# Eight weight slots and a third Strassen pair in a two-layer float32 trunk

## The chip, the core and the metric

The kernel runs on one core of one Trainium2 chip. Its time is that of the device in microseconds; lower is better. A core has TensorE (PE, matrix products), VectorE (DVE), ScalarE (ACT), GpSimd (POOL, nearly idle here) and SyncE (SP, which issues nearly all DMAs here). Each engine works through its own instructions in order and waits on semaphores that others raise.

## The reference

Two layers on x of 256 tokens by 2048, all in float32. Layer 0 mixes tokens by sparse attention, layer 1 by a short gated convolution, and each has a SwiGLU block behind it:

```python
for i in range(DEPTH):                       # DEPTH = 2
    if i % 2 == 0:
        x = x + _dsa_mixer(_rmsnorm(x, attn_norm[j]), attn_w_in[j], ..., attn_w_out[j])
    else:
        x = x + _shortconv_mixer(_rmsnorm(x, conv_norm[j]), conv_w_in[j], conv_w[j], conv_w_out[j])
    x = x + _swiglu(_rmsnorm(x, ffn_norm[i]), ffn_w_gate[i], ffn_w_up[i], ffn_w_down[i])

def _swiglu(h, w_gate, w_up, w_down):
    return (jax.nn.silu(h @ w_gate) * (h @ w_up)) @ w_down
```

w_gate and w_up are 2048 x 5632, w_down is 5632 x 2048. The weights make up nearly all of the 398 MB that are read from memory.

## The kernel before

**A float32 product in three.** Every operand is split in a high part (a rounding to the type float32r) and a low part (what is left). A product is then high x high + high x low + low x high: three matmuls of 128 x 128 on 512 columns (`product`, L726 to L728; `stream_rows`, L502 to L504, in the projections). ACT makes a weight's high part w_hi (L931), DVE its low part w_lo (L1282).

**Slots.** Weights come in slots of 128 partitions x 1024 numbers (512 KB), which is two row tiles of 512 columns. SP loads a slot into `stage`, ACT and DVE split it into w_hi and w_lo, PE uses it. All three buffers have RING = 4 places. SP may load slot n when slot n-4 has its low part (`lo_done`); ACT may write w_hi of slot n when PE is done with slot n-4 (`slot_used`).

**Units of gate and up.** A SwiGLU block has 11 units of 512 hidden columns (BLOCKS). A unit has eight pairs of slots, kp = 0 to 7; the even slot holds two row tiles of w_gate, the odd one the same rows of w_up. A plain pair (`plain_slot`, twice) is 2 slots x 2 token halves x 2 row tiles x 3 = 24 matmuls. The sums stand in the eight banks of PSUM, named P1 to P8. Units 1 to 10 are a loop on every engine.

**Mixed pairs.** Pairs 3 and 6 (MIXED_PAIRS) are done by a Strassen form: seven products in place of eight, so 21 matmuls (`mixed_pair`). Four of the products take the slots themselves, three take sums of weight quarters. DVE makes these sums from `stage` into t_raw with four subtractions (`mix_weights`, L1612 to L1617; the second, L1613, writes into `stage`), ACT makes t_hi (L1164), DVE t_lo (L1622, semaphore `t_ready`). t_raw, t_hi and t_lo exist once: the next mix waits for `t_used`, which PE raises with the pair's last product. The mixed inputs lie in sx, two sets, in the last four tiles of hs; they are made once a layer, from quarter j of the residual (`mix_x`, `mixed_x_high`, `mixed_x_low`).

**End of a unit.** During slots 0 to 3 of the next unit, ACT takes P1, DVE adds up the mixed sums (`take_mixed`, L1566), then gate (L1581) and up (L1586) rows, ACT does silu, DVE the product (`hid`, L1593). PE transposes the hidden block between slots 2 and 3 into banks 6 and 7 (`turn_hidden`, L536), which are also the banks P6 and P7 of the mixed pairs. ACT and DVE bring it as high and low part into hs (L1157, L1600, semaphore `hidden_ready`).

**Down.** Two passes of 44 slots on w_down, pairs 6, 9, 12, 15, 18 mixed. In the first pass the mixed forms of the hidden blocks are made as well, one set every six slots, behind t_lo: DVE (L1669 to L1678), ACT (L1196, L1198), DVE (L1684, L1685).

The order on every engine is written out by hand: `unit_slots` goes through the slots, and a table of steps says what follows a slot's split.

Of the kernel before, what the change touches and what calls it, by code (L numbers as in the profile page):

```python
# [32 lines left out]
P = 128  # L33
# [9 lines left out]
RING = 4  # L43
SLOT = 1024
# [21 lines left out]

def trunk(nc, x, attn_w_in, attn_w_out, conv_w_in, conv_w_out, w_gate, w_up, w_down,
          gains, head_gains, conv_taps, tables, mats, bounds, out):
    with ExitStack() as ctx:
# [7 lines left out]
        stage = sb("stage", [P, RING, SLOT])  # L77
# [6 lines left out]
        taps = sb("taps", [P, 3, KT])  # L84
        mat = sb("mat", [P, 2, P])
# [19 lines left out]
        sb("cross_square_sums", [P, 3, 4 * TOK])  # L105
        hgain = sb("hgain", [P, 2])
# [13 lines left out]
        mat_a = sb("mat_a", [P, 5, P], stack=part)  # L120
# [32 lines left out]
        sb("hs_but_last_block", [P, FT - 4, 2 * TOK], F32R, stack=tail_part)  # L153
        sx = sb("sx", [P, 2, 4, TOK], F32R, stack=tail_part)
# [27 lines left out]
        IDENT, MEAN_D = (mat[:, i, :] for i in range(2))  # L182
        MEAN_H, ROT_H, ROT_I, DUP, DUP_ROT = (mat_a[:, i, :] for i in range(5))
# [5 lines left out]
        loaded = [sem(f"loaded{i}") for i in range(RING)]  # L189
# [140 lines left out]
        MIXED_PAIRS = (3, 6)  # L330
# [13 lines left out]
        LAYER_MIXED = BLOCKS * FFN_MIXED + 2 * DN_MIXED  # L344
# [13 lines left out]
        def _(sp):  # L358
            def load(n, pos, rows_of, width):

                k = rows_of.shape[0] // P
                if not isinstance(n, int) or n >= RING:

                    sp.wait_ge(lo_done, n - (RING - 1))
                dst = stage[:, pos, 0:k * width].rearrange("p (k n) -> p k n", k=k)
                sp.dma_start(dst, rows_of.rearrange("(k p) n -> p k n", p=P)).then_inc(loaded[pos], 16)

            def load_block(n, w, base, col, width, tiles):

                per = SLOT // width if width >= NARROW else 4  # L370
                for s in range(tiles // per):
                    load(n + s, s % RING, w[s * per * P:(s + 1) * per * P, base:][:, bass.ds(col, width)], width)
# [6 lines left out]
            sp.dma_start(mat.ap(), mats[:, 0:2, :]).then_inc(in_ident, 16)  # L379
# [26 lines left out]
            def load_wide(first, w, tiles):  # L406

                slots = tiles // 2
                with sp.Fori(0, 2) as i:
                    for u in range(2):  # L410
                        for s in range(slots):
                            load(first + 2 * slots * i + u * slots + s, (u * slots + s) % RING,
                                 w[s * 2 * P:(s + 1) * 2 * P, WIDE * u:][:, bass.ds(2 * WIDE * i, WIDE)], WIDE)

            def load_ffn(first, layer):
                with sp.Fori(0, BLOCKS) as i:
                    for s in range(KT // 2):
                        rows2 = slice(2 * s * P, 2 * (s + 1) * P)
                        for side, w in enumerate((w_gate[layer], w_up[layer])):
                            j = 2 * s + side  # L420
                            load(first + 16 * i + j, j % RING, w[rows2, :][:, bass.ds(WIDE * i, WIDE)], WIDE)

            def load_down(first, layer):
                with sp.Fori(0, 2) as i:
                    for j, (s, side) in enumerate(DOWN_SLOTS):
                        rows2 = slice(2 * s * P, 2 * (s + 1) * P)
                        load(first + FT * i + j, j % RING,
                             w_down[layer][rows2, WIDE * side:][:, bass.ds(2 * WIDE * i, WIDE)], WIDE)
# [4 lines left out]
            for i in range(4):  # L433
                for u, base in enumerate((D, 2 * D, 0)):
                    load_block(S_CV + 24 * i + 8 * u, conv_w_in, base, WIDE * i, WIDE, KT)
# [15 lines left out]
        def _(pe):  # L451
# [69 lines left out]
            def stat(no):  # L521

                pe.wait_ge(stat_sum, 3)
                for a in range(2):
# [208 lines left out]
            def x_mixed(kp, s, form):  # L733
                return sx[:, s, form, 0:P], sx[:, s, form, P:TOK]
# [24 lines left out]
            def mixed_pair(n, kp, mixed_pairs, count, operand, mixed_operand, bank_free):  # L759
# [5 lines left out]
                if first:  # L765
                    for bank in (P1, P5, P6, P7):
# [6 lines left out]
                product(P5, mixed_operand(kp, s, 0), *half_slot(u, 0), first, last).then_inc(slot_used, 1)  # L773
                pe.wait_ge(t_ready, count + s + 1)
# [22 lines left out]
            def ffn(layer, first, q):  # L797
# [9 lines left out]
                def body(i, first_time):  # L807
# [7 lines left out]
                    for kp in range(KT // 2):  # L815
                        if first_time and kp % 2 == 0:
                            pe.wait_ge(xs_ready, 4 * q + kp // 2 + 1)
                        if kp in MIXED_PAIRS:
                            mixed_pair(n, kp, MIXED_PAIRS, LAYER_MIXED * layer + FFN_MIXED * i, xs, x_mixed, bank_free)
# [8 lines left out]
                with pe.Fori(1, BLOCKS) as i:  # L828
                    body(i, False)

            def down(layer, first):
                blocks = BLOCKS * (layer + 1)
                for u in range(2):
# [14 lines left out]
                    for j, (kp, side) in enumerate(DOWN_SLOTS):  # L848
# [3 lines left out]
                        elif side == 0:  # L852
                            if u == 0:
                                pe.wait_ge(mixed_hidden_ready, DN_MIXED * layer + DN_PAIRS.index(kp) + 1)
                            mixed_pair(n, kp, DN_PAIRS, LAYER_MIXED * layer + BLOCKS * FFN_MIXED + DN_MIXED * u, hs,
# [1035 lines left out]
```

## Time and profile before

| what | us |
|---|---|
| median of 3 runs | 2152.84 |
| lowest and highest | 2151.3 and 2156.05 |
| the profiled execution: its own time | 2151.01 |
| its span in the profile | 2149.2 |
| PE busy | 2125.5 (99%) |
| DVE busy | 1581.0 (74%) |
| ACT busy | 1144.1 (53%) |
| granted TensorE clock, share of full | 0.998 |

The span is from the first to the last instruction of the program. Busy time of an engine counts what it executes, not its waits. The end of a matmul in the profile is modelled, so the starts tell more than the ends. In the rows, the idle time in brackets is that of the engine before the instruction, and the arrow names what ended it. DMA moved 187 GB/s on average and its engines were busy for about six tenths.

### The profile page before, as it was taken

How to read it: one execution, taken by the hardware profiler on the slowest of the kernel's cores; microseconds unless marked ns; L12 is line 12 of the kernel's file. 1: busy time of each engine (PE TensorE's matmuls, PEld its weight loads, DVE VectorE, ACT ScalarE, POOL GpSimd, SP SyncE). 2: the span in 40 equal slices, each digit the busy share in tenths (PEclk: the TensorE clock that was granted, in tenths of full speed). 3: DMA queues.
4: the chain of work that ended last, by engine and by line, in shares of the span. 5: the costliest groups of instructions: out<-in, count | busy, mean ns of one | idle time of the engine just before them, and what ended most of it. 6: DMA issues, size and time to landing. Idle time of an engine off the chain costs nothing.

```text
span 2149.2 us, 28376 instructions
## 1 busy us (share of the span) xinstructions
PE 2125.5 (99%) x9834; PEld 1761.7 (82%) x9834; DVE 1581.0 (74%) x1758; ACT 1144.1 (53%) x1285; POOL 15.5 (1%) x14
## 2 busy tenths in 40 slices
PE   8999999999999999999999999999999999999999
PEld 7888888888888888788888888888888888887787
DVE  6887756888778877777755555568888888877776
ACT  5465655655565554454454444555655565544443
POOL 0001000000000000000000000000000000000000
PEclk9999999999999999999999999999999999999999
DMA  7555366666666665566666666666666666665665
GB/s 235 157 141 149 121 179 185 203 188 196 202 189 185 196 209 178 175 198 196 198 185 193 187 187 187 186 183 200 186 204 194 196 186 200 192 190 171 197 196 175
DMA packets 234761, 401.57 MB, mean 187 GB/s; under 512 B 15041, under 2 KB 56129, under 8 KB 234689
## 3 DMA queue, kind: packets, MB, share of 16 engines
q1 hardware_dynamic: 233824, 399.30, 61.4%
q10 hardware_dynamic: 864, 1.30, 0.2%
q8 instruction: 46, 0.75, 0.1%
q14 instruction: 27, 0.21, 0.0%
HBM read 398.45 MB, written 2.10 MB: 186 GB/s over the span
## 4 chain that ended last, share of the span: by engine, by line
PE 93%; DVE 4%; issue 1%; ACT 1%; DMA 1%; SPq 0%; ACTq 0%; DVEq 0%
PE ps L726 20%; PE ps L728 20%; PE ps L727 20%; PE ps L503 7%; PE ps L502 7%; PE ps L504 7%; PE ps L473 6%; PE ps L478 3%; PE ps L536 2%; DVE w_lo L1282 1%; ACT w_hi L931 0%; DMA stage<-in_w_down 0%; PE ps L654 0%; DVE t_lo L1622 0%; PE ps L592 0%
## 5 line engine op out<-in xcount | busy, mean ns | idle before, releaser
L931 ACT ACTIVATE w_hi<-stage 128x1024 fp32r<-128x1024 f32 x748 | 788.0, 1059 | 876.8 <-PE ps L728 557.4
L1282 DVE TENSOR_TENSOR w_lo<-stage,w_hi 128x1024 fp32r<-128x1024 f32 x748 | 906.1, 1222 | 381.9 <-ACT w_hi L931 370.9
L726 PE MATMUL ps<-w_hi,xs 128*128 128x512 f32 x1184 | 462.7, 391 | 0.0
L727 PE MATMUL ps<-w_lo,xs 128*128 128x512 f32 x1184 | 461.3, 390 | 0.0
L728 PE MATMUL ps<-w_hi,xs 128*128 128x512 f32 x1184 | 460.9, 389 | 0.0
L728 PEld LDWEIGHTS ps<-w_hi,xs 128*128 128x128 f32 x1184 | 222.3, 188 | 46.5
L726 PEld LDWEIGHTS ps<-w_hi,xs 128*128 128x128 f32 x1184 | 222.3, 188 | 46.3
L727 PEld LDWEIGHTS ps<-w_lo,xs 128*128 128x128 f32 x1184 | 222.3, 188 | 45.7
L726 PE MATMUL ps<-w_hi,hs 128*128 128x512 f32 x584 | 230.7, 395 | 10.2 <-DVE w_lo L1282 10.2
L728 PE MATMUL ps<-w_hi,hs 128*128 128x512 f32 x584 | 229.2, 392 | 0.0
L727 PE MATMUL ps<-w_lo,hs 128*128 128x512 f32 x584 | 229.1, 392 | 0.0
L473 PE MATMUL ps<-xs,w_hi 128*128 128x512 f32 (+1 forms) x528 | 169.4, 403 | 0.0
L502 PE MATMUL ps<-w_hi,xs 128*128 128x512 f32 x384 | 150.2, 391 | 0.0
L504 PE MATMUL ps<-w_hi,xs 128*128 128x512 f32 x384 | 149.5, 389 | 0.0
L503 PE MATMUL ps<-w_lo,xs 128*128 128x512 f32 x384 | 149.4, 389 | 0.0
L726 PEld LDWEIGHTS ps<-w_hi,hs 128*128 128x128 f32 x584 | 110.8, 190 | 36.4 <-DVE w_lo L1282 12.7
L728 PEld LDWEIGHTS ps<-w_hi,hs 128*128 128x128 f32 x584 | 110.6, 189 | 23.5
L727 PEld LDWEIGHTS ps<-w_lo,hs 128*128 128x128 f32 x584 | 110.9, 190 | 23.1
L1622 DVE TENSOR_TENSOR t_lo<-t_raw,t_hi 128x1536 fp32r<-128x1536 f32 x64 | 112.3, 1755 | 5.8 <-ACT t_hi L1164 4.2
L478 PEld LDWEIGHTS ps<-xs,w_lo 128*128 128x128 f32 (+1 forms) x528 | 96.3, 187 | 21.3
L1612 DVE TENSOR_TENSOR t_raw<-stage 128x512 f32<-128x512 f32 x64 | 44.3, 692 | 86.6 <-DMA stage<-in_w_up 42.1
L478 PE MATMUL ps<-xs,w_lo 128*128 128x256 f32 (+1 forms) x528 | 102.7, 279 | 0.0
(202 smaller groups left out, 2406.4 us busy)
## 6 DMA issues: line engine op xcount, KB each, us to landing
stage<-in_w_gate SPq DMA_DIRECT2D x176, 512.0 KB, 3.8
stage<-in_w_up SPq DMA_DIRECT2D x176, 512.0 KB, 4.3
stage<-in_w_down SPq DMA_DIRECT2D x176, 512.0 KB, 4.5
stage<-in_conv_w_in SPq DMA_DIRECT2D x96, 512.0 KB, 4.0
stage<-in_attn_w_in SPq DMA_DIRECT2D x48, 512.0 KB, 3.8
stage<-in_attn_w_out SPq DMA_DIRECT2D x32, 512.0 KB, 4.3
stage<-in_conv_w_out SPq DMA_DIRECT2D x32, 512.0 KB, 3.7
stage<-in_attn_w_in SPq DMA_DIRECT2D x32, 256.0 KB, 3.4
```

The source lines that it names most:

```text
L473: return pe.matmul(ps[0:count, banks[m], :], w_hi[:, slot, at], rhs, start=k == 0, stop=last)
L478: return pe.matmul(ps[0:count, banks[m], TOK:], w_lo[:, slot, at], rhs[:, 0:TOK], start=False, stop=False)
L502: pe.matmul(bank, hi, w_hi[:, slot, cols], start=k == 0, stop=False)
L503: pe.matmul(bank, hi, w_lo[:, slot, cols], start=False, stop=False)
L504: mm = pe.matmul(bank, lo, w_hi[:, slot, cols], start=False, stop=k == tiles - 1)
L726: pe.matmul(ps[:, bank, :], hi, b_hi, start=start, stop=False)
L727: pe.matmul(ps[:, bank, :], hi, b_lo, start=False, stop=False)
L728: return pe.matmul(ps[:, bank, :], lo, b_hi, start=False, stop=stop)
L931: nc.scalar.activation(w_hi[:, j % RING, :], stage[:, j % RING, :], ACT.Copy).then_inc(hi_done, 1)
L1282: tt(w_lo[:, p, :], stage[:, p, :], f32(w_hi[:, p, :]), ALU.subtract).then_inc(lo_done, 1)
L1612: tt(t3, b22, b12, ALU.subtract).then_inc(t_step, 1)
L1622: tt(t_lo[:, :, :], t_raw[:, :, :], f32(t_hi[:, :, :]), ALU.subtract).then_inc(t_ready, 1)
```

## The change

- `stage` gets eight places (DEEP). From the attention's output projection on (slot S_AO) SP loads slot n when slot n-8 has its low part; w_hi and w_lo keep four places. `stage_at` gives the place, `landed` the value of its semaphore.
- MIXED_PAIRS becomes (2, 4, 6), and LAST_MIXED = (2, 6) holds for the last unit of each layer, which is written out behind the loop. sx gets three sets, in the last six tiles of hs.
- The mixed inputs are now made from quarters 1, 2 and 3 of the residual. The hidden block's high and low part come after slot 5 of the next unit, ahead of t_hi and t_lo of pair 2 (`between`), and PE waits for P6 and P7 only ahead of the products that write them.
- Room is made: MEAN_D moves from `mat` to the matrices that are loaded later, and the descriptor space that the program reserves is cut from its default to 512 bytes per partition.
- SP's loads of w_down are written out instead of looped.

```diff
-        stage = sb("stage", [P, RING, SLOT])
+        stage = sb("stage", [P, DEEP, SLOT])
...
+def stage_at(n):
+    return n % RING if n < S_AO else (n - S_AO) % DEEP
+
+
+def landed(n, loop_slots=0, i=0):
+    if n < S_AO:
+        return 16 * (n // RING + 1) + 16 * (loop_slots // RING) * i
+    sooner = S_AO // RING if stage_at(n) < RING else 0
+    return 16 * (sooner + (n - S_AO) // DEEP + 1) + 16 * (loop_slots // DEEP) * i
...
-        MIXED_PAIRS = (3, 6)
+        MIXED_PAIRS = (2, 4, 6)
+        LAST_MIXED = (2, 6)
+        FORM_PLACE = {4: 0, 2: 1, 6: 2}
...
+        ALL_FFN_MIXED = (BLOCKS - 1) * FFN_MIXED + len(LAST_MIXED)
+        LAYER_MIXED = ALL_FFN_MIXED + 2 * DN_MIXED
+
+        def mixed_of(i):
+            return LAST_MIXED if isinstance(i, int) and i == BLOCKS - 1 else MIXED_PAIRS
...
-            def load(n, pos, rows_of, width):
+            def load(n, pos, rows_of, width, depth=RING):
...
-                if not isinstance(n, int) or n >= RING:
-
-                    sp.wait_ge(lo_done, n - (RING - 1))
+                if not isinstance(n, int) or n >= depth:
+
+                    sp.wait_ge(lo_done, n - (depth - 1))
...
                 if first:
-                    for bank in (P1, P5, P6, P7):
+                    for bank in (P1, P5):
                         bank_free(bank)
...
+                if first:
+                    bank_free(P6)
+                    bank_free(P7)
                 pe.wait_ge(t_ready, count + s + 1)
...
-                with pe.Fori(1, BLOCKS) as i:
+                with pe.Fori(1, BLOCKS - 1) as i:
                     body(i, False)
+                body(BLOCKS - 1, False)
...
                     if s is not None and j % 2:
+                        if s == 0 and between is not None:
+                            between()
                         mixed_high(count + s)
...
-                        if s == 0 and after_sums is not None:
-                            after_sums()
                     split(first, 1, per_loop, i, j)
                     if s is not None and j % 2:
+                        if s == 0 and between is not None:
+                            between()
                         mixed_low(count + s)
```

How the instructions stand on DVE in the loop of gate and up, from the third slot's low part on: L1612 to L1617 is a mix, L1600 the hidden block's low part, L1622 t_lo. Before:

```order
324 L1282 TENSOR_TENSOR w_lo<-stage,w_hi 128x1024
325 L1606 ISA
326 L1612 TENSOR_TENSOR t_raw<-stage 128x512
327 L1613 TENSOR_TENSOR stage<-stage 128x512
328 L1614 REGISTER_ALU
329 L1615 TENSOR_TENSOR t_raw<-stage 128x512
330 L1616 ISA
331 L1617 TENSOR_TENSOR t_raw<-stage,t_raw 128x512
332 L1600 ISA
333 L1600 REGISTER_ALU
334 L1600 TENSOR_TENSOR hs<-ps,hs 128x4x256
335 L1280 REGISTER_ALU
```

And after, where L1646 to L1651 are the mix, L1634 the hidden block's low part and L1656 t_lo:

```order
340 L1651 TENSOR_TENSOR t_raw<-stage,t_raw 128x512
341 L1312 REGISTER_ALU
342 L1314 TENSOR_TENSOR w_lo<-stage,w_hi 128x1024
343 L1312 REGISTER_ALU
344 L1314 TENSOR_TENSOR w_lo<-stage,w_hi 128x1024
345 L1634 ISA
346 L1634 REGISTER_ALU
347 L1634 TENSOR_TENSOR hs<-ps,hs 128x4x256
348 L1656 TENSOR_TENSOR t_lo<-t_raw,t_hi 128x1536
```

The hidden block's low part stood between the mix and the pair's two w_lo; it now stands between the two w_lo and t_lo, and the mix is that of pair 2 instead of pair 3. The same on DVE in a layer's first unit, from the last addition to the residual (L1344) on. Before, with L1315 the low part of the scaled inputs:

```order
266 L1344 TENSOR_TENSOR res<-res,ps 128x2x512
267 L1282 TENSOR_TENSOR w_lo<-stage,w_hi 128x1024 x2
268 L1612 TENSOR_TENSOR t_raw<-stage 128x512
269 L1613 TENSOR_TENSOR stage<-stage 128x512
270 L1615 TENSOR_TENSOR t_raw<-stage 128x512
271 L1617 TENSOR_TENSOR t_raw<-stage,t_raw 128x512
272 L1282 TENSOR_TENSOR w_lo<-stage,w_hi 128x1024
273 L1315 TENSOR_TENSOR xs<-total,xs 128x4x256
```

And after, with L1379 the addition and L1347 the low part of the scaled inputs:

```order
272 L1379 TENSOR_TENSOR res<-res,ps 128x2x512
273 L1646 TENSOR_TENSOR t_raw<-stage 128x512
274 L1647 TENSOR_TENSOR stage<-stage 128x512
275 L1649 TENSOR_TENSOR t_raw<-stage 128x512
276 L1651 TENSOR_TENSOR t_raw<-stage,t_raw 128x512
277 L1314 TENSOR_TENSOR w_lo<-stage,w_hi 128x1024 x2
278 L1656 TENSOR_TENSOR t_lo<-t_raw,t_hi 128x1536
279 L1314 TENSOR_TENSOR w_lo<-stage,w_hi 128x1024
280 L1347 TENSOR_TENSOR xs<-total,xs 128x4x256
```

The first mix moved ahead of two w_lo, and t_lo ahead of the scaled inputs' low part, behind which a second mix now follows (rows 287 to 290, not shown).

## Rows read from the trace of the kernel before

**Rows 1.** Page, part 1: busy time, share of the span, instructions

```profile
PE 2125.5 (99%) x9834; PEld 1761.7 (82%) x9834; DVE 1581.0 (74%) x1758; ACT 1144.1 (53%) x1285; POOL 15.5 (1%) x14
```

**Rows 2.** Waits of PE: total us, times, longest us

```profile
PE ps L726 <- DVE w_lo L1282: 10.2, 7, 2.4
```

**Rows 3.** Timeline of PE, one gate/up unit: start us, us, engine line

```profile
736.65 0.39 PE L726 MATMUL ps<-w_hi,xs 128*128 128x512 f32 x1
...
739.37 0.39 PE L726 MATMUL ps<-w_hi,xs 128*128 128x512 f32 x1
...
744.82 1.04 PE L536 MATMUL ps<-mat,total 128*128 128x128 f32 x8
745.61 0.48 PE L726 MATMUL ps<-w_hi,xs 128*128 128x512 f32 x1
...
755.23 0.39 PE L726 MATMUL ps<-w_hi,sx 128*128 128x512 f32 x1
...
756.59 0.39 PE L726 MATMUL ps<-t_hi,sx 128*128 128x512 f32 x1
...
758.69 0.39 PE L726 MATMUL ps<-w_hi,xs 128*128 128x512 f32 x1
...
779.87 0.39 PE L726 MATMUL ps<-w_hi,xs 128*128 128x512 f32 x1
```

**Rows 4.** Timeline of DVE, the same unit; in brackets idle time and its end

```profile
739.34 1.22 DVE L1282 TENSOR_TENSOR w_lo<-stage,w_hi 128x1024 fp32r<-128x1024 f32 x1
740.47 1.41 DVE L1593 SCALAR_TENSOR_TENSOR total<-total,rs,gated 128x512 f32<-128x512 f32 x2
741.80 1.22 DVE L1282 TENSOR_TENSOR w_lo<-stage,w_hi 128x1024 fp32r<-128x1024 f32 x1
...
744.75 0.69 DVE L1612 TENSOR_TENSOR t_raw<-stage 128x512 f32<-128x512 f32 x1
...
747.42 1.22 DVE L1600 TENSOR_TENSOR hs<-ps,hs 128x1024 f32 x1
748.55 2.40 DVE L1282 TENSOR_TENSOR w_lo<-stage,w_hi 128x1024 fp32r<-128x1024 f32 x2
751.10 1.76 DVE L1622 TENSOR_TENSOR t_lo<-t_raw,t_hi 128x1536 fp32r<-128x1536 f32 x1
752.78 1.22 DVE L1282 TENSOR_TENSOR w_lo<-stage,w_hi 128x1024 fp32r<-128x1024 f32 x1
...
760.45 0.69 DVE L1612 TENSOR_TENSOR t_raw<-stage 128x512 f32<-128x512 f32 x1 [1.35 <-DMA stage<-in_w_up]
...
774.61 0.69 DVE L1566 TENSOR_TENSOR total<-ps,gated 128x512 f32<-128x512 f32 x1
...
777.61 1.22 DVE L1581 TENSOR_TENSOR gated<-gated,ps 128x1024 f32<-128x1024 f32 x1
778.75 1.22 DVE L1282 TENSOR_TENSOR w_lo<-stage,w_hi 128x1024 fp32r<-128x1024 f32 x1
780.07 1.22 DVE L1586 TENSOR_TENSOR total<-total,ps 128x1024 f32<-128x1024 f32 x1
```

**Rows 5.** Timeline of ACT, the same unit

```profile
739.57 1.06 ACT L931 ACTIVATE w_hi<-stage 128x1024 fp32r<-128x1024 f32 x1 [0.78 <-PE ps L728]
...
746.00 1.03 ACT L1157 ACTIVATE hs<-ps 128x1024 f32 x1
...
749.60 1.47 ACT L1164 ACTIVATE t_hi<-t_raw 128x1536 fp32r<-128x1536 f32 x1
```

**Rows 6.** Timeline of ACT, DVE and PE in layer 0's first down pass

```profile
882.78 1.06 ACT L931 ACTIVATE w_hi<-stage 128x1024 fp32r<-128x1024 f32 x1 [2.25 <-DMA stage<-in_w_down]
...
886.02 0.69 DVE L1612 TENSOR_TENSOR t_raw<-stage 128x512 f32<-128x512 f32 x1 [3.00 <-issue]
...
894.58 0.53 ACT L1196 ACTIVATE xs<-total 128x384 fp32r<-128x384 f32 x1 [4.29 <-DVE total L1678]
...
896.28 1.23 DVE L1282 TENSOR_TENSOR w_lo<-stage,w_hi 128x1024 fp32r<-128x1024 f32 x1 [1.80 <-ACT w_hi L931]
...
897.56 0.80 PE L726 MATMUL ps<-w_hi,hs 128*128 128x512 f32 x1 [2.44 <-DVE w_lo L1282]
```

More of the change, by code:

```diff
@@ L43 @@
 RING = 4
+DEEP = 8
 SLOT = 1024
@@ L411, in load_wide @@
                         for s in range(slots):
[L412 to L413 removed]
+                            load(first + 2 * slots * i + u * slots + s, (u * slots + s) % DEEP,
+                                 w[s * 2 * P:(s + 1) * 2 * P, WIDE * u:][:, bass.ds(2 * WIDE * i, WIDE)], WIDE,
+                                 RING if u == 0 and s < RING else DEEP)
             def load_ffn(first, layer):
@@ L1281, in split @@
                     p = j % RING
-                    tt(w_lo[:, p, :], stage[:, p, :], f32(w_hi[:, p, :]), ALU.subtract).then_inc(lo_done, 1)
+                    tt(w_lo[:, p, :], stage[:, stage_at(first + j), :], f32(w_hi[:, p, :]), ALU.subtract).then_inc(lo_done, 1)
             def steps_between(first, slots, steps, per_loop=0, i=0, at=0):
@@ L1622, in mixed_low, with unit_slots @@
                 tt(t_lo[:, :, :], t_raw[:, :, :], f32(t_hi[:, :, :]), ALU.subtract).then_inc(t_ready, 1)
-            def unit_slots(first, slots, mixed_pairs, count, steps, per_loop=0, i=0, ahead=None, after_sums=None):
+            def unit_slots(first, slots, mixed_pairs, count, steps, per_loop=0, i=0, ahead=None, between=None):
                 for j in range(slots):
@@ L1650, in unit_steps, with unit, later_unit @@
                             3: [lambda: hid(done + i, q)]}
-                def unit(i, steps, ahead, after_sums=None):
-                    unit_slots(first, 16, MIXED_PAIRS, LAYER_MIXED * layer + FFN_MIXED * i, steps, 16, i, ahead, after_sums)
-                unit(0, before, lambda: dve.wait_ge(res_squared, 4 + 8 * q))
-                with dve.Fori(1, BLOCKS) as i:
+                def unit(i, steps, ahead, between=None):
+                    unit_slots(first, 16, mixed_of(i), LAYER_MIXED * layer + FFN_MIXED * i, steps, 16, i, ahead, between)
+                def later_unit(i):
                     unit(i, unit_steps(i - 1), lambda: dve.wait_ge(hid_made, 2 * (done + i)),
@@ L1659, in ffn @@
                 last = BLOCKS - 1
+                unit(0, before, lambda: dve.wait_ge(res_squared, 4 + 8 * q))
+                with dve.Fori(1, last) as i:
+                    later_unit(i)
+                later_unit(last)
                 return merged(unit_steps(last), {6: [lambda: hidden_low(done + last, last)]})
```

111 lines of the change are left out of this document (59 added, 52 removed).

## The prediction

> **What bounds the kernel now.** I read the page first: TensorE (PE) is busy for 2125.5 of 2149.2 us [rows 1], so only two kinds of gain exist, fewer matmuls or fewer of the 23.7 us in which PE stands. Next the waits of PE: almost all that is left after the start of the program is one line, seven waits of an L726 matmul for a low half w_lo, 10.2 us together [rows 2]. Then the timeline of one gate/up unit, on PE [rows 3], VectorE (DVE) [rows 4] and ScalarE (ACT) [rows 5], because there the change adds DVE work to a stage in which PE now never stops; and last a stretch of the down projection, where the seven waits lie [rows 6].
>
> A unit starts on PE at 736.65 and the next at 779.87: 43.22 us. A slot of 12 products takes 2.72 us (736.65 to 739.37), so 0.227 us a matmul, and a plain pair 5.44. In a mixed pair six products on the slots take 1.36 us (755.23 to 756.59), and the nine on t_hi and t_lo take 2.10 (756.59 to 758.69), slightly slower each at 0.233. A mixed pair is thus 1.36 + 1.36 + 2.10 = 4.82 us. The eight transposes of the hidden block hold PE for 0.79 (744.82 to 745.61) [rows 3].
>
> **Part 1: 20 more mixed pairs.** Before, each of 2 x 11 units has two; after, ten of eleven have three and the last two, so 64 for 44. Each new one takes 24 matmuls away and puts 21 in: 5.44 - 4.82 = 0.62 us. 20 x 0.62 = **12.4 us**, all of it on PE, which sets the end there. A unit would last 43.22 - 0.62 = 42.60.
>
> Whether PE can take it depends on DVE. I use the distance from start to start where DVE stands in nothing [rows 4]: w_lo 1.13 (739.34 to 740.47), the two products of hid 1.33 (740.47 to 741.80), the four subtractions of a mix 2.67 (744.75 to 747.42), the hidden block's low half 1.13 (747.42 to 748.55), t_lo 1.68 (751.10 to 752.78), the four additions of a take 3.00 (774.61 to 777.61), the gate rows 1.14 (777.61 to 778.75), the up rows about 1.3 (1.22 and a wait for its own end). A unit after is 16 x 1.13 + 3 x (2.67 + 1.68) + 3.00 + 1.14 + 1.3 + 1.33 + 1.13 = 39.0 us, before 34.7. So 3.6 us of the 42.6 are spare in sum, and the question is where they lie. Two chains decide, and I lay them out from the unit's start on PE (0). PE reaches slot 4 at 11.69 (four slots of 2.72 and the turn), needs t_lo of pair 2 at 14.41, ends that pair at 16.51, needs t_lo of pair 4 at 24.68, ends it at 26.78, and needs that of pair 6 at 34.95.
>
> First chain, from one mixed pair to the next. t_raw, t_hi and t_lo exist once, so DVE mixes slot 8 only when PE has let go of pair 2. A release shows on ACT 0.20 us after PE's next start (739.37, 739.57 [rows 3, 5]). From there 0.20 + 2.67 + 2 x 1.13 for two w_lo + 1.76 for t_lo to its end = 6.9 us, and ACT's t_hi (1.47 [rows 5], it starts when the mix is done, 2.9 after the release) fits below the two w_lo. PE comes for it one plain pair and one slot later, 5.44 + 2.72 = 8.16. Spare: **1.2 us**, the same between pairs 4 and 6. Before, two plain pairs lay between the mixed ones and this chain was slack by over 6 us.
>
> Second chain, from the turn to pair 2. The hidden block is transposed into banks 6 and 7, which pair 2 then needs. The transposes end near 9.2; ACT's high half 1.03 (746.00 [rows 5]) brings 10.2, t_hi 1.47 brings 11.7, t_lo 1.76 brings 13.5, needed at 14.41: **0.9 us** spare. The DVE side of it: the up rows from 0.2 on, two w_lo, hid, gives a mix from 5.1 to 7.8, two w_lo to 10.1, the hidden low half behind ACT to 11.4; it is not the later one. The hidden row needs the turn at 8.17, and hid ends at 5.1. DVE then has w_lo 6 and 7 done at 15.7, before it may mix again at 16.7, so it does not fall behind; at the end of the unit it does the take at 37.3 to 40.3, gate rows to 41.4, w_lo, and is ready for the up rows when PE hands them over. The cycle closes.
>
> What is late next is therefore t_lo, by about 1 us the other way. In the very first unit of each layer DVE also has the last quarter of the residual and one more set of mixed inputs in the same place. That leaves some half a us for pair 4; I price it at 0 to 1 us for each of two layers and take 0. The two inputs mixed earlier, in the projections, are four additions of 128x128 and one low half while DVE has a slot's work of 1.13 in each 2.72; they cost nothing. P6 and P7 are now waited for after slot 5 rather than before slot 4, which can only help.
>
> **Part 2: eight slots.** It takes out no instruction. DMA issues stand in SP's queue, each behind a w_lo; the wait is now for the w_lo seven back rather than three. In the down projection a mix waits 3.00 us (886.02) for its second slot, and ACT for its first (882.78, 2.25) [rows 6]. Then follow, in order, two w_lo, t_lo, the mixed hidden block, ACT's part of it (894.58, which had waited 4.29), w_hi, w_lo (896.28), and PE, which had stood 2.44 us, starts at 897.56. From the mix to that w_lo's end it is 886.02 to 897.51 = 11.5 us, in which PE does the mixed pair without a stop: it is the slot behind it that comes late. With the load in eight slots ahead the mix starts up to 3.0 us sooner, more than any of the waits (2.4 the longest [rows 2]). What is next: slot 13's high half waits for slot 9 to be free; by the same pitches w_lo 14 is then there 0.9 us before PE. DVE has 15.5 us of work and waits in each three pairs, PE 2 x 5.44 + 4.82 = 15.7, so it keeps up, narrowly. So all seven go: 10.2 us, and 7 x 0.16 more, since the idle time is counted from a modelled end 0.39 after the last start where the next matmul would come after 0.227. **11.3 us.** Bounds: 0 (the mixed block alone is enough) to 11.3.
>
> In the gate/up loop the mix also waited for a load (760.45, 1.35 [rows 4]); PE did not wait for it, so its end gives nothing by itself, but without it the first chain above would not fit: 6.9 + 1.35 = 8.25 against 8.16.
>
> **Part 3: the rest.** MEAN_D comes with the later small loads, and PE waits for them before its first use; DVE already waits for the same semaphore before the slots ahead of it, so nothing. The first DMA is half as large: a gain of a few tenths at most, taken as 0. The reserved descriptor space serves software queues, and the page lists none. Unrolled last units add code, of the kind that the down projection already runs without a stop.
>
> **A rule that speaks against it.** The trace shows a 1.22 us w_lo followed by the next start after 1.13 [rows 4]. The Trainium skill, "VectorE: DVE Perf Modes", section "The DRAIN you can't avoid", has the next operation wait until the pipe is empty, which read strictly is a pitch of at least the duration; the trace does not agree.
>
> **Sum.** 12.4 + 11.3 = 23.7 us. The profiled execution took 2151.0, so 2127.3; the median of the three runs is 1.8 above it, and on that scale it is 2152.8 - 23.7 = **2129 us**.
>
> **Rivals.**
> - *DVE sets the unit.* If operations followed each other by their full times, a unit would be 16 x 1.22 + 3 x (4 x 0.69 + 1.76) + 4 x 0.69 + 2 x 1.22 + 1.41 + 1.22 = 40.9, plus the two stands of about 1 us in which DVE may not mix yet: 43.0 or more, so part 1 gives nothing and the time is 2152.8 - 11.3 = 2141. For it: DVE was already at 35 of 43 us. Against: rows 4. This is also what the skill's rule named above comes to.
> - *The waits in down stay.* The mixed hidden block holds ACT (4.29) and the next w_hi, whatever the loads do. Then 2152.8 - 12.4 = 2140. For it: ACT's wait is the longest of the stretch. Against: it starts when the mix starts, and that waited for DMA.
> - *Slower.* The second chain: PE stands in front of bank 6 or t_lo of pair 2 in each of the 20 units that turn a hidden block. It has 0.9 us to spare and costs 20 us for each us beyond; it outweighs the gain from 2.1 us late on (1.2 x 20 = 24). If ACT or DVE did one w_lo and one t_lo more than I think before it (1.13 + 1.76 = 2.9), 2.0 x 20 = 40 us: 2169. For it: five instructions on three engines in series, moved forward by a pair. Against: each has its row.
> - *The change does less than it says.* Loads still arrive one by one, if SP is held by something else: the first chain misses by 0.1 us twice in 20 units and the down waits stay, 2144.
>
> **How the numbers follow.** Forecast 0.76, DVE bound 0.08, down waits 0.07, slower 0.06, less 0.03. A difference below 0.2% (4.3 us) can't be told from none here. The three middle cases are faster; a mixture that ends within 0.2% gets 0.03, slower 0.06, so faster 0.91. Range: the low end 2125 is the forecast less the run-to-run spread and the start; the high end 2143 takes in the rivals at 2140 and 2141, as the slack in both chains is 1 us and a miss of 0.3 us in 20 units, three times, would be 18.
>
> **What would show it.** Right: units of 42.6 us, 9774 matmuls, no PE wait in the first down halves, t_raw waiting for PE and no longer for DMA. Wrong: PE waiting for t_lo or for the hidden low half once per unit (rival one or three), or for w_lo after a mixed hidden block (rival two).

## The result and the profile after

The changed kernel takes 2117.07 us (median of 4 runs, 2116.89 to 2117.97) and the kernel before, beside it, 2154.45 (4 runs, 2151.3 to 2156.64): a ratio of 0.9828, 95% interval 0.9811 to 0.9845. The sign was as forecast, and so were the two gains that the prediction counted. The size was not: 37.4 us between the medians where 23.7 were forecast, and 2117.1 lies below the range of 2125 to 2143. Between the two profiled executions (2151.0 and 2116.9) the difference is 34.1 us; it is that difference which is taken apart below.

Page of the kernel after, part 1 (busy time, share, instructions) and the line that sums the chain of waits:

```profile
PE 2101.6 (99%) x9774; PEld 1749.1 (83%) x9774; DVE 1657.3 (78%) x1868; ACT 1160.5 (55%) x1303; POOL 15.4 (1%) x14
...
PE 98%; DVE 1%; ACT 0%; issue 0%; DMA 0%; SPq 0%; DVEq 0%; ACTq 0%
```

Against [rows 1]: 9834 - 9774 = 60 matmuls fewer, three for each of 20 pairs, and 76 us more of DVE (1581.0 to 1657.3), for which PE never waits in gate, up or down. What PE still waits for (total us, times, longest):

```profile
PE ps L557 <- DMA res<-in_x: 5.9, 1, 5.9
...
PE ps L684 <- DVE prob L1558: 1.4, 1, 1.4
```

The line of [rows 2], seven waits for w_lo, is gone, and nothing has come in its place: what is left is the start of the program and the attention (rows of 2.4, 0.4 and 0.2 us are not shown). DVE's waits changed as forecast: t_raw waits for PE to let go of the last mixed pair, and no longer for a load.

```profile
DVE w_lo L1314 <- ACT w_hi L957: 303.1, 236, 4.4
DVE t_raw L1646 <- PE ps L749: 40.7, 36, 1.2
```

One gate/up unit on PE (start us, us, engine line), the answer to [rows 3]:

```profile
730.50 0.39 PE L747 MATMUL ps<-w_hi,xs 128*128 128x512 f32 x1
...
738.67 1.04 PE L557 MATMUL ps<-mat,total 128*128 128x128 f32 x8
...
745.03 0.39 PE L747 MATMUL ps<-t_hi,sx 128*128 128x512 f32 x1
...
747.07 0.39 PE L747 MATMUL ps<-w_hi,xs 128*128 128x512 f32 x1
...
748.43 0.39 PE L747 MATMUL ps<-w_hi,xs 128*128 128x512 f32 x1
...
755.23 0.39 PE L747 MATMUL ps<-t_hi,sx 128*128 128x512 f32 x1
...
772.91 0.39 PE L747 MATMUL ps<-w_hi,xs 128*128 128x512 f32 x1
```

The unit lasts 772.91 - 730.50 = 42.41 us where 42.60 were forecast. The nine products on t_hi and t_lo take 747.07 - 745.03 = 2.04 us, 0.2267 each; in [rows 3] they took 2.10, 0.2333 each. That small difference is the first of the two terms that were missing. The same unit on DVE, where the two chains can be read:

```profile
742.29 1.76 DVE L1656 TENSOR_TENSOR t_lo<-t_raw,t_hi 128x1536 fp32r<-128x1536 f32 x1
743.96 2.35 DVE L1314 TENSOR_TENSOR w_lo<-stage,w_hi 128x1024 fp32r<-128x1024 f32 x2
747.37 0.69 DVE L1646 TENSOR_TENSOR t_raw<-stage 128x512 f32<-128x512 f32 x1 [1.05 <-PE ps L749]
...
752.30 1.75 DVE L1656 TENSOR_TENSOR t_lo<-t_raw,t_hi 128x1536 fp32r<-128x1536 f32 x1
```

Second chain: t_lo of pair 2 ends at 742.29 + 1.76 = 744.05 and PE wants it at 745.03, 0.98 us spare (forecast 0.9). First chain: PE lets go at 747.07, DVE mixes at 747.37, t_lo of pair 4 ends at 754.05, and PE wants it at 755.23: 1.18 us spare (forecast 1.2). In the later units of the loop it is the same, 0.95 to 0.98 and 1.17 to 1.18 us. Early in a layer there is less. The second chain has 0.91 and 0.76 us (layer 0 and layer 1) in the first unit that turns a hidden block. In a layer's very first unit pair 4 has 0.79 and 0.82, where the prediction left some half a us, and pair 6 has 0.63 and 0.86.

The clock in five stretches of before, and then in two of them after. Columns: stretch, sum, busy time (instructions) of PE, PEld, DVE, ACT, POOL, granted clock, DMA share, GB/s.

```profile
890.00:900.00 10.00, 7.56 (x28) 5.75 (x28) 8.10 (x12) 4.80 (x7) 0.00 (x0) 0.87 0.44 130
900.00:910.00 10.00, 10.00 (x44) 8.20 (x43) 7.19 (x9) 3.62 (x3) 0.00 (x0) 0.95 0.61 188
1950.00:1960.00 10.00, 8.00 (x34) 6.22 (x33) 8.10 (x12) 5.70 (x7) 0.00 (x0) 0.95 0.37 109
1960.00:1970.00 10.00, 10.00 (x41) 8.10 (x40) 7.00 (x9) 3.62 (x3) 0.00 (x0) 0.88 0.63 206
1990.00:2000.00 10.00, 7.69 (x27) 5.78 (x27) 7.44 (x12) 4.52 (x6) 0.00 (x0) 0.83 0.48 158
```

```profile
890.00:900.00 10.00, 10.00 (x46) 8.29 (x45) 7.99 (x11) 5.05 (x7) 0.00 (x0) 1.00 0.67 224
...
1990.00:2000.00 10.00, 10.00 (x46) 8.29 (x45) 6.20 (x6) 4.24 (x4) 0.00 (x0) 1.00 0.49 151
```

Before, the down passes ran with the full clock of 2.4 GHz except in three places, each behind one of the longer stops: the slices around them read 0.83 to 0.95. After, with no stop, these two and the other three read 1.00. That is the second missing term. The start of the program goes the other way: from 10 to 20 us the granted clock was 1.00 in the profiled execution of before and 0.83 in that of after.

### The profile page after: what moved, and what is told of

The parts are those of the page before. It is cut to its first block, busy times and chain, and to the rows that moved or that the text cites. A ratio compares the mean times of both kernels' runs of the same rounds, so it can differ in the third digit from the quotient of the medians.

```text
span 2115.1 us, 27861 instructions
## 1 busy us (share of the span) xinstructions
PE 2101.6 (99%) x9774; PEld 1749.1 (83%) x9774; DVE 1657.3 (78%) x1868; ACT 1160.5 (55%) x1303; POOL 15.4 (1%) x14
## 4 chain that ended last, share of the span: by engine, by line
PE 98%; DVE 1%; ACT 0%; issue 0%; DMA 0%; SPq 0%; DVEq 0%; ACTq 0%
PE ps L747 22%; PE ps L749 22%; PE ps L748 22%; PE ps L524 7%; PE ps L522 7%; PE ps L523 7%; PE ps L493 6%; PE ps L498 3%; PE ps L557 2%; PE ps L675 0%; PE ps L613 0%; PE ps L684 0%; PE ps L665 0%; DMA res<-in_x 0%; DVE w_lo L1314 0%
## 5 line engine op out<-in xcount | busy, mean ns | idle before, releaser
L1314 DVE TENSOR_TENSOR w_lo<-stage,w_hi 128x1024 fp32r<-128x1024 f32 x748 | 895.8, 1221 | 309.2 <-ACT w_hi L957 303.1
L747 PE MATMUL ps<-w_hi,xs 128*128 128x512 f32 x1064 | 416.0, 391 | 0.0
L749 PE MATMUL ps<-w_hi,xs 128*128 128x512 f32 x1064 | 414.3, 389 | 0.0
L748 PE MATMUL ps<-w_lo,xs 128*128 128x512 f32 x1064 | 414.0, 389 | 0.0
L749 PEld LDWEIGHTS ps<-w_hi,xs 128*128 128x128 f32 x1064 | 199.7, 188 | 41.7
L748 PEld LDWEIGHTS ps<-w_lo,xs 128*128 128x128 f32 x1064 | 199.9, 188 | 40.8
L747 PEld LDWEIGHTS ps<-w_hi,xs 128*128 128x128 f32 x1064 | 199.8, 188 | 40.7
L747 PE MATMUL ps<-w_hi,hs 128*128 128x512 f32 x584 | 227.6, 390 | 0.0
L749 PE MATMUL ps<-w_hi,hs 128*128 128x512 f32 x584 | 227.2, 389 | 0.0
L522 PE MATMUL ps<-w_hi,xs 128*128 128x512 f32 x384 | 150.2, 391 | 0.0
L1656 DVE TENSOR_TENSOR t_lo<-t_raw,t_hi 128x1536 fp32r<-128x1536 f32 x84 | 147.5, 1755 | 3.0 <-ACT t_hi L1190 2.1
L524 PE MATMUL ps<-w_hi,xs 128*128 128x512 f32 x384 | 149.5, 389 | 0.0
L523 PE MATMUL ps<-w_lo,xs 128*128 128x512 f32 x384 | 149.4, 389 | 0.0
L1190 ACT ACTIVATE t_hi<-t_raw 128x1536 fp32r<-128x1536 f32 x84 | 124.6, 1483 | 13.6 <-DVE t_raw L1651 13.6
```

The source lines that it names most:

```text
L522: pe.matmul(bank, hi, w_hi[:, slot, cols], start=k == 0, stop=False)
L523: pe.matmul(bank, hi, w_lo[:, slot, cols], start=False, stop=False)
L524: mm = pe.matmul(bank, lo, w_hi[:, slot, cols], start=False, stop=k == tiles - 1)
L747: pe.matmul(ps[:, bank, :], hi, b_hi, start=start, stop=False)
L748: pe.matmul(ps[:, bank, :], hi, b_lo, start=False, stop=False)
L749: return pe.matmul(ps[:, bank, :], lo, b_hi, start=False, stop=stop)
```

## The experiments

All edits are to the kernel after, unless the text says otherwise. Ratios are to the kernel before.

**The slots alone.** Every unit keeps two mixed pairs, in places 2 and 6, as the last unit of the change has them. The mixing of the inputs for a third pair stays, unused.

```diff
-        MIXED_PAIRS = (2, 4, 6)
+        FORM_PAIRS = (2, 4, 6)
+        MIXED_PAIRS = (2, 6)
```

> The changed kernel with its eight slots, but two mixed pairs (2 and 6) in every gate/up unit; the third set of mixed inputs is made and not used. Theory A (the gain is the matmuls of 20 pairs, plus the down waits and a slow clock behind them, plus a faster pitch of the products that stream t_hi and t_lo): 20 pairs come back at 3 matmuls of 0.227 us each, 13.6 us above the changed kernel's 2117.1, so 2130.7, units of 43.1 us, no wait of PE in the down passes. Theory B (the eight slots themselves bring more than the down waits, elsewhere): the time stays nearer the changed kernel, below 2127. Theory C (the third pair brings more than its matmuls): above 2134.

Measured: 2130.73 us (2130.59 to 2130.98), ratio 0.989 (0.9873 to 0.9906), with no stop of PE in gate, up or down. The 20 pairs are thus worth 13.66 us, 20 x 3 x 0.227 = 13.6 to within a tenth. The forecast of 12.4 took the nine products at 0.233; at 0.2267 a mixed pair is 21 x 0.2267 = 4.76 and saves 0.68. The slots and all that came with them, the new order and the new addresses too, are worth 23.5 us (2154.26 beside it, less 2130.73) where 11.3 were forecast: the miss is there.

**The pairs with four slots.** The memory of `stage` stays eight places long; only four are used.

```diff
-DEEP = 8
+DEEP = 4
...
-        stage = sb("stage", [P, DEEP, SLOT])
+        stage = sb("stage", [P, 8, SLOT])
```

> The changed kernel with all its mixed pairs but loads only four slots ahead, as before. Theory A (the seven stops of PE in the first down passes come from the late load, and behind the longer ones PE runs at half clock for a while): the stops come back, 11.3 us, with 1.7 us more for each of about three slow stretches, 5; in gate and up a mix that waits 1.35 us for its load overruns the 1.2 us of slack by 0.1 to 0.5 in 40 places, 4 to 20 us. Together 2137 to 2153. Theory B (the mixed hidden block makes the stops, whatever the loads do, and they went for another reason): no stops in down, 2117 to 2125, all of it in gate and up.

Measured: 2146.84 us (2146.0 to 2149.48), ratio 0.9968 (0.9957 to 0.9979). Waits of PE, the first and the third row:

```profile
PE ps L747 <- DVE w_lo L1314: 11.1, 6, 2.5
...
PE ps L747 <- DVE gated L1615: 4.9, 10, 1.5
```

Waits of DVE in the same execution:

```profile
DVE t_raw L1646 <- issue: 24.2, 8, 3.6
DVE t_raw L1646 <- DMA stage<-in_w_down: 18.3, 10, 2.5
```

The down stops are back with the shallow slots, six of them, and t_raw waits for loads again. In the gate/up units PE stops too, as the expectation has it, but in another place: not for t_lo, but at the unit's start for the gate rows (L1615). One unit's end on ACT and DVE shows the way there:

```profile
644.01 1.28 ACT L957 ACT_TABLE_LOAD   x1 [1.50 <-DMA stage<-in_w_gate]
...
646.39 1.23 DVE L1314 TENSOR_TENSOR w_lo<-stage,w_hi 128x1024 fp32r<-128x1024 f32 x1 [1.33 <-ACT w_hi L957]
647.53 0.69 DVE L1600 TENSOR_TENSOR total<-ps,gated 128x512 f32<-128x512 f32 x1
...
650.53 1.22 DVE L1615 TENSOR_TENSOR gated<-gated,ps 128x1024 f32<-128x1024 f32 x1
```

ACT waits 1.50 us for a load and then has a table load of 1.28 us ahead of that w_hi; DVE waits 1.33 us for it, and the take and the gate rows stand behind that w_lo in DVE's order. They end at 651.75 and PE starts at 651.81. What ACT waits for in that execution:

```profile
ACT w_hi L957 <- DMA stage<-in_w_gate: 36.0, 40, 1.6
```

The waits of ACT in the kernel after have no row of that kind. From start to start all stops, those too short for a row of their own too, make 20.4 us and the matmuls that follow at a slower pitch 8.0 (against the same count in the kernel after), so 28.4 of the 31.1 us between the two profiled executions, and 1.5 lie in the start of the program. Three stretches at half clock are among them, behind stops of 2.40, 2.46 and 2.36 us in the down passes; behind the one of 2.25 there is none. So the third pair needs the eight slots. The ratio of 0.9968 is 7.4 us, but 4.1 of these come from an address that this kernel has as well (measured on the kernel before, in the experiment after next), so with four slots the pairs and their new order gain 3.3 us (2150.14 less 2146.84); with eight the pairs bring 13.7. The slots do not need the pairs: alone they brought most of the gain.

**The small tile back in its place.** `taps` is a tile of 192 bytes per partition. The change moved its declaration from ahead of the tiles t_raw, t_hi and t_lo to behind them. With the other sizes ahead of them multiples of 256 (`mat` went from 1024 to 512 bytes, the descriptor space from its default to 512), these three moved from 192 bytes past a multiple of 256 to a multiple. The description of the change ahead of the prediction does not name this line of the diff. `mat`, `total` and the tiles behind it move along with the three.

```diff
         gain = sb("gain", [P, 4, KT])
+        taps = sb("taps", [P, 3, KT])
...
-        taps = sb("taps", [P, 3, KT])
```

> The changed kernel with one line moved back: the 192-byte tile taps stands again ahead of t_raw, t_hi and t_lo in SBUF, so these begin at a multiple of 64 bytes and no longer at one of 256. Nothing else moves (hs and sx keep their places, since taps stood right behind). Theory A (the address of the streamed operand sets the pitch): the nine products of a mixed pair go back from 0.2267 to 0.2333 us each, 84 pairs x 9 x 0.0067 = 5.1 us: 2122.2. Theory B (the pitch got faster for another reason, the eight slots or less traffic): no change, 2117.1, pitch 0.2267.

Measured: 2123.53 us (2123.1 to 2124.02), ratio 0.9856 (0.984 to 0.9873), 6.5 us more than after. No stop has come; the products on t are slower. Groups by line, operation and tile (busy us, mean ns of one): before, two rows of the same stage,

```profile
L726 PE MATMUL ps<-t_hi,sx 128*128 128x512 f32 x88 | 34.7, 394 | 0.0
...
L726 PE MATMUL ps<-w_hi,sx 128*128 128x512 f32 x88 | 34.2, 389 | 0.0
```

after,

```profile
L747 PE MATMUL ps<-t_hi,sx 128*128 128x512 f32 x128 | 49.8, 389 | 0.0
```

and with the tile moved back:

```profile
L747 PE MATMUL ps<-t_hi,sx 128*128 128x512 f32 x128 | 50.4, 394 | 0.0
```

The durations are modelled; by the starts the pitch is 0.2333 us against 0.2267. 84 mixed pairs x 9 x 0.0067 = **5.1 us**. The other 1.4 us of the 6.5 (units of 42.62 us) lie right behind the nine products: over the 84 pairs the next six matmuls take 1.38 us on average with the tile back and 1.36 after, and 84 x 0.02 = 1.7 is of that size. In the kernel before it is the same. With [rows 3], where the nine end at 758.69, and with 747.07 and 748.43 above:

```profile
760.07 0.39 PE L726 MATMUL ps<-w_hi,xs 128*128 128x512 f32 x1
```

That is 760.07 - 758.69 = 1.38 us before and 748.43 - 747.07 = 1.36 after. Why matmuls on w_hi and w_lo should still be late there is not shown. In the rows of before the difference of the nine also stands between t_hi and w_hi in the same pair: same shape, same sx, 394 and 389 ns. The transposes that read `mat` and `total` account for about 0.1 us of the difference, so the move shows on the products on t and those behind them.

**The same move alone, in the kernel before.** Its two mixed pairs, four slots and sizes stay; only `taps` goes behind the t tiles.

```diff
-        taps = sb("taps", [P, 3, KT])
...
+        taps = sb("taps", [P, 3, KT])
         hgain = sb("hgain", [P, 2])
```

> The kernel before with that one line moved: taps behind t_raw, t_hi and t_lo, which then begin at a multiple of 256 bytes. Theory A (address): 64 pairs x 9 x 0.0067 = 3.8 us less than the kernel before, pitch 0.2267 in the mixed products. Theory B (other cause): no change, pitch 0.2333. The stops in down stay in both.

Measured: 2150.14 us (10 runs, 2148.68 to 2152.01), ratio 0.9982 (0.9972 to 0.9992): 4.1 us faster than the 2154.26 beside it, with one line moved. The group of the same line, which now shows 389 ns:

```profile
L726 PE MATMUL ps<-t_hi,sx 128*128 128x512 f32 x88 | 34.2, 389 | 0.0
```

The seven stops of [rows 2] have stayed, so they are not what was gained. In the profiled execution they are even longer (12.2 us for 10.2) and the start of the program takes 1.3 us more, so that it lies only 1.0 us below the profiled one of before; the rest of its matmuls make up the 4.3 us between.

**Two other addresses.** Is it the 192 bytes, or any place off a multiple of 256? The first puts the t tiles 128 bytes past it, the second 64, and `total` and the tiles behind it with them; the rest stays at multiples of 256. Each is a single execution.

```diff
+        sb("pad_one", [P, 32])
...
+        sb("pad_two", [P, 32])
...
-    nc = bacc.Bacc("TRN2", target_bir_lowering=False, num_devices=1, dynamic_dma_scratch_size=512)
+    nc = bacc.Bacc("TRN2", target_bir_lowering=False, num_devices=1, dynamic_dma_scratch_size=256)
```

> The changed kernel with t_raw, t_hi and t_lo 128 bytes further on, so that they begin at an odd multiple of 128; hs and all else stay at multiples of 256. Theory A (a streamed operand must begin at a multiple of 128 bytes): pitch 0.2267 us as in the changed kernel, 2117. Theory B (it must be one of 256): pitch 0.2333, 2122 to 2123.

> The changed kernel with t_raw, t_hi and t_lo 64 bytes further on (an odd multiple of 64), all else at multiples of 256. At 192 bytes past a multiple of 256 the mixed products took 0.2333 us, at 128 past 0.233 on average with an uneven beat, at 0 past 0.2267. Theory A (only a multiple of 256 is fast): 0.233, 2122 to 2124. Theory B (the loss grows with the distance): between 0.2267 and 0.2333, 2119 to 2121.

Measured: 2124.46 us at 128 bytes and 2124.11 at 64 (there the pads are 16 and 48 elements). The same group, two lines further down in these kernels, at 128 and then at 64:

```profile
L749 PE MATMUL ps<-t_hi,sx 128*128 128x512 f32 x128 | 50.8, 396 | 0.0
```

```profile
L749 PE MATMUL ps<-t_hi,sx 128*128 128x512 f32 x128 | 50.7, 396 | 0.0
```

Of the four residues tried, 0, 64, 128 and 192, only 0 is fast; the other three cost about the same 7 us of the whole. They do not cost it in the same place. From the first of the nine products to the matmul behind them it is 2.04 us at 0, 2.10 at 192 and at 128, but 2.08 at 64 (0.2308 each), and there the next twelve matmuls lose more, 2.77 us for 2.72. So at 64 the time is that of "only a multiple of 256 is fast" and the pitch of the nine lies in between, as theory B had it.

**How much slack the first chain has.** The prediction gave 1.2 us from the end of one mixed pair to t_lo of the next. To test it, DVE gets extra work ahead of t_lo of pair 4 in each of the 20 units (and of pair 6 in the last unit of a layer, where there is room): first one reduction of 512 columns, then two of 1024. `delay` is called ahead of `mixed_low` where s is 1; the operation waits on the semaphore of the one before.

```diff
+            def delay(i, count):
+                layer = 1 if first_layer_done else 0
+                for m in range(2):
+                    at = 2 * (BLOCKS * layer + i) + m
+                    if not isinstance(at, int) or at:
+                        dve.wait_ge(delayed, at)
+                    nc.vector.tensor_reduce(junk[:, 0:2], t_raw[:, 0:2, :], AX_X, ALU.add).then_inc(delayed, 1)
```

> The changed kernel with one more DVE operation of 512 columns (about 0.7 us, a sum that nobody reads) in front of t_lo of the second mixed pair of every gate/up unit. Theory A (the chain from the end of one mixed pair to t_lo of the next has 1.2 us to spare, as the trace of the changed kernel also shows): nothing is lost, 2117.1 within 0.5. Theory B (DVE, at 39 us of work in 42.4, is what sets the unit's length): 20 units of 0.7 us, 2131.

> As the one before, but with two such operations of 1024 columns, about 2.5 us with the waits between them. Theory A: 2.5 - 1.2 = 1.3 us of stop in each of the 20 units with pair 4, with 0.16 to resume: 2117 + 29 = 2146, PE waiting for t_lo at pair 4 only, and no slow clock behind stops this short. Theory B (DVE's sum sets the unit): 41.5 us of work still fits 42.4 plus its waits, a loss of 2.5 a unit, 2167.

Measured: 2117.33 us (2115.82 to 2118.15), ratio 0.9827 (0.9811 to 0.9844), with one, and 2146.79 (2144.56 to 2147.33), ratio 0.9965 (0.9953 to 0.9978), with two. The wait of PE with two:

```profile
PE ps L748 <- DVE t_lo L1667: 22.8, 20, 1.5
```

Both came within 1 us of the expectation. One operation disappears in the 1.18 us of slack, of which the trace still shows 0.58; two stop PE 20 times, 1.26 us each from start to start and 1.65 and 1.61 in the first unit of either layer, 26.0 in all. So the working of the first chain holds in both directions: 1.2 us spare, and 20 us for each us beyond it. The second chain, from the turn of the hidden block to pair 2, was not lengthened in any run.

**Longer stops, twenty times.** The same with three operations of 1024 columns, to ask what a stop of 2.5 us costs beyond its own length.

```diff
-                for m in range(2):
+                for m in range(3):
```

> As before with three operations of 1024 columns, 3.7 us: PE stops 2.5 us in each of 20 units. Theory A (a stop of 2 us or more makes PE run at half clock for some eight matmuls afterwards, whatever the stage; in the kernel before that followed the stops of 2.0, 2.3 and 2.4 us and none of 1.7 or less): 20 x (2.5 + 0.16 + 1.7) = 87 us, 2204, and a granted clock clearly under 1 in gate and up. Theory B (the slow stretches in down had another cause than the stops): 20 x 2.7 = 53, 2170.

Measured: 2184.54 us (2184.33 to 2185.43), ratio 1.0142 (1.0125 to 1.0159). It is between the two theories and confirms neither. The wait, and two of the twenty places (columns as above; the second row of each pair is the stretch behind the stop):

```profile
PE ps L748 <- DVE t_lo L1667: 47.8, 20, 2.7
```

```profile
372.00:378.00 6.00, 3.30 (x15) 2.40 (x14) 5.93 (x5) 1.54 (x3) 0.00 (x0) 1.00 0.50 170
378.00:384.00 6.00, 6.00 (x21) 4.77 (x20) 4.80 (x8) 3.71 (x4) 0.00 (x0) 0.72 0.61 171
421.00:427.00 6.00, 3.65 (x17) 2.68 (x16) 5.74 (x6) 0.21 (x1) 0.00 (x0) 1.00 0.29 75
427.00:433.00 6.00, 6.00 (x28) 4.98 (x27) 5.93 (x7) 4.84 (x5) 0.00 (x0) 1.00 0.65 222
```

The first unit's stop, 2.70 us, is followed by a clock of 0.72 and 21 matmuls in 6 us; the next unit's, 2.35 us in the same place, by 1.00 and 28. Of the 20 stops 8 were followed by a stretch at half clock: the two of 2.70 and 2.74 us, and six of the eighteen that lasted 2.35 or 2.36. They account for the time: 20 x 2.55 = 51.0 of stops and 8 x 1.7 = 13.6 of clock make 64.6 of the 67.5 us over the kernel after. What tells the six from the twelve of the same length stays open.

**The kernel before, again.** Two more executions of the kernel before, without an edit, to see whether its own runs differ by these stops and by the clock.

> The kernel before, profiled again. Its runs lie between 2150.4 and 2157.0, those of the changed kernel within about a microsecond or two, and the profile that the prediction read is of an execution of 2151.0. Theory A (the spread comes from the stops in down and how often half clock follows them, 1.7 us each): an execution near 2154 shows more or longer stops, or five or six slow stretches where that one showed three. Theory B (the spread is elsewhere, such as in the start): the sum of stops and slow stretches is the same, 15 to 17 us, whatever the time.

> The kernel before, a second time, with the same two expectations: by theory A stops and slow stretches together differ between executions by as much as their times, by theory B they do not.

Measured: 2153.83 and 2151.96 us. The same row of PE's waits, in the first and in the second:

```profile
PE ps L726 <- DVE w_lo L1282: 11.2, 7, 2.4
```

```profile
PE ps L726 <- DVE w_lo L1282: 10.8, 7, 2.4
```

One of the stops in the first of them, on PE (start, duration, and in brackets the idle time and its end):

```profile
899.58 0.50 PE L726 MATMUL ps<-w_hi,hs 128*128 128x512 f32 x1 [2.24 <-DVE w_lo L1282]
...
900.15 0.63 PE L728 MATMUL ps<-w_hi,hs 128*128 128x512 f32 x1
900.58 0.63 PE L726 MATMUL ps<-w_hi,hs 128*128 128x512 f32 x1
901.00 0.63 PE L727 MATMUL ps<-w_lo,hs 128*128 128x512 f32 x1
```

And the clock around it:

```profile
894.00:900.00 6.00, 3.76 (x17) 2.76 (x16) 4.10 (x9) 3.40 (x5) 0.00 (x0) 1.00 0.43 158
900.00:906.00 6.00, 6.00 (x21) 4.79 (x20) 3.60 (x4) 2.17 (x3) 0.00 (x0) 0.72 0.71 188
```

After a stop of 2.24 us the next starts are 0.43 apart (900.15, 900.58, 901.00) where 0.227 is the pitch at full clock: 1.2 GHz instead of 2.4. It lasts for some eight matmuls, 8 x 0.2 = 1.6 us and 0.1 at its edges, 1.7 in all. In all three executions of the kernel before that I have a trace of there are three such stretches in the down passes. Eleven of the 21 stops in them had 1.8 us of idle time or more, and nine of these were followed by half clock, the shortest of 1.83 us; one of 2.41 and one of 1.81 were not, nor was any of the ten of 1.7 or less. 3 x 1.7 = **5.1 us**.

So the slow stretches were the same in number, and the second theory is right about them. The stops differ, 10.2, 11.2 and 10.8 us in executions of 2151.0, 2153.8 and 2152.0, and so does the start of the program: in the first of these two it has a stretch at half clock and takes 1.6 us more than in the profiled execution of before, in the second 0.1. Each theory has a part of it.

## Why the prediction was wrong

By the steps of the prediction, between the profiled executions:

| Term | Forecast | Measured | How |
|---|---|---|---|
| 20 more mixed pairs, at the old pitch | 12.4 | 12.4 | 42.60 forecast for the unit, 42.62 with the tile back |
| seven stops, start to start | 11.3 | 11.3 | no stop after; [rows 2] |
| products on t_hi and t_lo | 0 | 5.1 | 84 x 9 x 0.0067, tile back and tile moved alone |
| the matmuls right behind them | 0 | 1.7 | 84 x 0.02, starts before and with the tile back |
| half clock behind three stops | 0 | 5.1 | 3 x 1.7, clock of the stretches |
| start of the program | 0 | -1.3 | PE is past its wait for prob at 267.50 before, 268.75 after |
| sum | 23.7 | 34.3 of 34.1 | |

The start goes against the change in this pair of executions by what looks like chance: in the traces its length varies from one execution to the next, by 1.6 us between those of the kernel before alone.

**What held.** That PE sets the end; the unit; both chains, each within 0.1 us; the 9774 matmuls; that all seven stops go; and in down the slack behind the mixed pair, which was put at 0.9 us. There w_lo ends at 869.05 (867.82 + 1.23) and PE starts on its slot at 869.93. DVE, ACT and PE in that stretch of after, the answer to [rows 6]:

```profile
867.82 1.23 DVE L1314 TENSOR_TENSOR w_lo<-stage,w_hi 128x1024 fp32r<-128x1024 f32 x1 [1.80 <-ACT w_hi L957]
```

```profile
866.11 0.53 ACT L1228 ACTIVATE xs<-total 128x384 fp32r<-128x384 f32 x1 [3.67 <-DVE total L1716]
```

```profile
869.93 0.39 PE L747 MATMUL ps<-w_hi,hs 128*128 128x512 f32 x1
```

ACT still waits 3.67 us for the mixed hidden block (4.29 in [rows 6]) and DVE 1.80 for w_hi, as the second rival said; only the whole chain now starts early enough, so that PE does not notice. The rival "DVE sets the unit" fell with the unit of 42.41 us and with the experiment in which a whole extra operation of DVE cost nothing. The slower rival fell by the trace: the second chain, on which it rests, has 0.76 us or more in each of the 20 units, and PE waits for t_lo in none of them; how it would behave with less was not tried. The rival of loads that arrive late fell with the first chain, which has its 1.2 us, and with DVE, which no longer waits for a load there.

**The step that failed first: "So all seven go: 10.2 us, and 7 x 0.16 more".** It priced a stop at the time that PE stands, and the term had its size wrong: 11.3 us, where the stops with what follows them measured 16.4. A stop does not end there: the next eight matmuls run at half clock after three of the seven. Nothing needed to be guessed for that. The granted clock of the five stretches above was in the trace of before, the table ahead of the prediction gives 0.998 for the whole, and the row of [rows 6] itself shows it: the matmul at 897.56 took 0.80 us where its like take 0.39. I cited the row for its wait and not for its duration. The Trainium skill, "TensorE: Matmul & The Clock Gate", section "HAM oscillation — how this bites in real kernels", says that PE, when it has waited long enough, starts its next work cold, which is at half rate; the trace agrees in kind, with 0.427 us a matmul for 0.227, and adds that here stops of 1.8 to 2.7 us were enough for some of them and not for all (9 of 11 in the three traces of before, 8 of 20 in the experiment).

**The step that failed second: part 3, "The rest", which priced the small moves at nothing.** It went through MEAN_D, the first DMA and the descriptor space, and did not speak of `taps` at all, which the diff moves. The prediction had even measured what it does: "slightly slower each at 0.233" stands in its first part. It took the 0.233 over into the new pairs as if it belonged to the products, so 5.1 us and the 1.7 behind them stood in the sum as nothing, and never asked why a matmul of the same shape takes 3% longer when its operand lies in another tile. Asked, the question has few answers (the operand's address, its other buffer, its writer), and the change touches the first.

**What stays open.** Between the medians the difference is 37.4 us, 3.3 more than between the profiled executions. The profiled execution of before (2151.0) is at the low end of the 17 runs beside the experiments (2150.42 to 2156.82, median 2154.26), and the prediction's scale, 1.8 us above it, was set by three runs. By the medians the surplus lies with the slots: from the kernel before with only the tile moved (2150.14) to the slots alone (2130.73) it is 19.4 us, where stops and half clock make 16.4. The trace of the former points the same way. It is of an execution near the median of its runs, and against the profiled one of before its stops are 2.0 us longer and its start 1.3. No execution of the kernel before above 2154 has a trace, so for that kernel it is not shown. After the change the runs lie within 1.1 us, which fits a kernel with no stops left whose length could vary, but that is argued and not tested.

## What to carry to other kernels

A stop of the engine that sets the end can cost more than its idle time: read the durations and the granted clock of the ten matmuls behind it, and count what they lose into the gain of removing it. Where two groups of the same operation and shape differ by a few ns in their means, find out why before the number goes into a sum; here it was an address, and one line moved gave 4 us in the old kernel. Every line of a diff that moves a tile's declaration changes the addresses of those behind it, so it deserves a term in the sum, even when its own work is nothing. And a sum that closes against one pair of profiled executions can close by luck: here the start of the program alone differed by 1.6 us between executions of the same kernel.

## What was not expected of the hardware

- A matmul with a streamed operand of 128x512 in fp32r starts each 0.2267 us if the operand's tile begins at a multiple of 256 bytes in the partition, and each 0.2333 at 192 bytes past one (389 and 394 ns in the means); 64 and 128 past it are slow as well (0.2308 and 0.2329), and the matmuls right behind such a run lose a little too. In this kernel it is 6.5 to 7.4 us of 2117. The Trainium skill, "SBUF — State Buffer", section "Operand start alignment", asks for a multiple of the element size alone and says that this concerns what is legal and not speed; nothing here contradicts it, and the runs supply the speed.
- A stop of PE of 1.8 to 2.7 us can be followed by some eight matmuls at 1.2 GHz (0.427 us each, 1.7 us lost), and equal stops in equal places are not always: 6 of 18 at 2.35 us. None of the 20 stops in the run with two operations was (1.10 to 1.49 us of idle time), nor any of 1.7 or less in the kernel before.
- From PE's next start to the DVE operation that waited for its release it is 0.30 us (747.07, 747.37) where I had taken the 0.20 that ACT shows in [rows 5].
